# Eight weight buffers moved to different addresses, and half of the matrix products run from the last column to the first

## What is computed

```
for i in range(2):
    x = LN(a*x + 0.5 * swiglu(x, w_gu[i,0], w_down[i,0]))      # 1024 -> 2 x 2816 -> 1024
    y = token_mix(x @ w_in[i]) @ w_out[i]                      # attention heads, recurrent heads
    x = LN(a*x + y)
    x = LN(a*x + 0.5 * swiglu(x, w_gu[i,1], w_down[i,1]))
    x = x + sigmoid(x @ w_g[i] + b_g[i]) * (p[i] @ w_p[i])
```

## Time and profile before

| | |
|---|---|
| median of 2 runs | 2225.23 us (2224.98 to 2225.49) |
| span of the profiled execution | 2226.4 us |
| PE busy | 2188.5 us, 98% of the span |
| weight loads (beside PE) | 1807.6 us, 81% |
| DVE, ACT, POOL busy | 1134.1, 902.1, 137.8 us |
| mean granted TensorE clock | 0.998 of 2.4 GHz |

### The profile page before, as it was taken

How to read it: one execution, slowest core, us unless ns; L and a number is a source line. 1 busy time by engine, 2 the same in 40 slices (tenths; PEclk the granted TensorE clock), 3 DMA queues, 4 the chain that set the end, 5 groups by cost and what they waited for, 6 DMA issues and landing times.

```text
span 2226.4 us, 30811 instructions
## 1 busy us (share of the span) xinstructions
PE 2188.5 (98%) x12675; PEld 1807.6 (81%) x12675; DVE 1134.1 (51%) x1966; ACT 902.1 (41%) x1447; POOL 137.8 (6%) x128
## 2 busy tenths in 40 slices
PE   9999999999999999999999999999999999999999
PEld 7888889877668888888888888898776788888888
DVE  4333345888867333343643333358887663333454
ACT  4223224555656322322632222255466462232234
POOL 0000011210001000012000000112200100000110
PEclk9999999999999999999999999999999999999999
DMA  5333333322222333332333333333322233333322
GB/s 167 97 102 95 88 95 90 99 65 70 81 72 67 104 95 98 106 89 85 107 95 95 100 100 86 98 80 99 77 67 67 67 95 96 101 98 97 95 88 72
DMA packets 384219, 202.76 MB, mean 91 GB/s; under 512 B 17360, under 2 KB 381776, under 8 KB 384080
## 3 DMA queue, kind: packets, MB, share of 16 engines
q1 hardware_dynamic: 383520, 200.15, 31.7%
q10 hardware_dynamic: 560, 0.66, 0.1%
HBM read 198.68 MB, written 2.10 MB: 90 GB/s over the span
## 4 chain that ended last, share of the span: by engine, by line
PE 82%; DVE 9%; ACT 6%; issue 2%; DMA 1%; POOL 0%; SPq 0%; DVEq 0%; ACTq 0%
PE banks L254 24%; PE banks L255 24%; PE banks L256 24%; DVE lev L1241 2%; ACT xhi L353 1%; PE banks L1518 1%; DVE w_lo L246 1%; DVE att L1277 1%; ACT lev L1121 1%; ACT w_hi L240 1%; ACT xT L354 1%; PE banks L1505 1%; PE banks L1459 1%; PE banks L305 1%; PE banks L311 1%
## 5 line engine op out<-in xcount | busy, mean ns | idle before, releaser
L246 DVE TENSOR_TENSOR w_lo<-w_raw,w_hi 128x1024 fp32r<-128x1024 f32 (+2 forms) x370 | 452.5, 1226 | 831.6 <-ACT w_hi L240 831.3
L254 PE MATMUL banks<-xhi,w_hi 128*128 128x512 f32 (+1 forms) x1936 | 758.1, 392 | 1.0 <-DVE w_lo L246 1.0
L256 PE MATMUL banks<-xhi,w_lo 128*128 128x512 f32 (+1 forms) x1936 | 749.7, 387 | 0.0
L255 PE MATMUL banks<-xlo,w_hi 128*128 128x512 f32 (+1 forms) x1936 | 749.7, 387 | 0.0
L240 ACT ACTIVATE w_hi<-w_raw 128x1024 fp32r<-128x1024 f32 (+2 forms) x370 | 376.0, 1018 | 810.0 <-PE banks L256 796.7
L254 PEld LDWEIGHTS banks<-xhi,w_hi 128*128 128x128 f32 x1936 | 365.6, 189 | 75.8 <-issue 1.6
L256 PEld LDWEIGHTS banks<-xhi,w_lo 128*128 128x128 f32 x1936 | 364.1, 188 | 74.6
L255 PEld LDWEIGHTS banks<-xlo,w_hi 128*128 128x128 f32 x1936 | 364.5, 188 | 72.5 <-issue 1.0
L254 PE MATMUL banks<-hhi,w_hi 128*128 128x512 f32 (+1 forms) x792 | 293.4, 371 | 0.0
L256 PE MATMUL banks<-hhi,w_lo 128*128 128x512 f32 (+1 forms) x792 | 289.5, 365 | 0.0
L255 PE MATMUL banks<-hlo,w_hi 128*128 128x512 f32 (+1 forms) x792 | 289.4, 365 | 0.0
(11 more groups left out here) (274 smaller groups left out, 2002.0 us busy)
## 6 DMA issues: line engine op xcount, KB each, us to landing
w_raw<-in_ffn_w_gu_dram SPq DMA_DIRECT2D x176, 512.0 KB, 4.0
w_raw<-in_ffn_w_down_dram SPq DMA_DIRECT2D x64, 512.0 KB, 4.0
w_raw<-in_w_in_dram SPq DMA_DIRECT2D x48, 512.0 KB, 4.1
w_raw<-in_ffn_w_down_dram SPq DMA_DIRECT2D x32, 384.0 KB, 3.5
w_raw<-in_w_out_dram SPq DMA_DIRECT2D x32, 256.0 KB, 2.9
w_raw<-in_ple_gate_w_dram SPq DMA_DIRECT2D x16, 512.0 KB, 3.7
w_raw<-in_cmp_k_w_dram SPq DMA_DIRECT2D x16, 256.0 KB, 2.8
w_raw<-in_cmp_v_w_dram SPq DMA_DIRECT2D x16, 256.0 KB, 3.2
```

Of the source, the lines that this page charges most:

```text
L246: dve.tensor_tensor(part_view(wlo, n), raw_view(split_at[n]).rearrange("p k n -> p (k n)"), part_view(whi, n), ALU.subtract).then_inc(sems ...
L254: pe.matmul(bank, w_hi, x_hi, start=first, stop=False)
L255: pe.matmul(bank, w_hi, x_lo, start=False, stop=False)
L256: return pe.matmul(bank, w_lo, x_hi, start=False, stop=last)
```

## The change

Two things change for the operands of the products.

**Addresses.** Each split buffer gets 64 bytes behind its 4096, so that the four buffers of `w_hi` begin 64 bytes apart modulo 512, and those of `w_lo` follow on: the eight begin at eight different residues modulo 512 (counted from the residue of the moving tiles: 0, 64, 128, 192 for `w_hi` and 256, 320, 384, 448 for `w_lo`). Room comes from `place`, which now reserves two bytes for a 2-byte element, and from `mask_b` and `ident_b` at their used width: 3072 bytes less, of which the buffers take 512. `w_raw` moves down by 3072 bytes and the working tiles behind the buffers by 2560, all by whole multiples of 512. ACT and DVE write the split pieces through a view of blocks (blocks x 128) in place of one run of the same elements, and read the raw piece in the same view.

**Direction.** In `multiply`, for pieces with `n // 4` odd, the moving tiles and the result bank are addressed with step -1: the first column that is read is column 511, and its result goes to column 511 of the bank. The weights are read as before. Nothing changes in what lands where. The other functions with products keep their direction.

```
-            at[0] += 4 * int(np.prod(shape[1:]))
+            at[0] += (2 if dt == BF16 else 4) * int(np.prod(shape[1:]))
...
-        mask_b = place(low, "mask_b", [P, 2 * (C_HG - C_MASK)], BF16)
-        ident_b = place(low, "ident_b", [P, 2 * P], BF16)
+        mask_b = place(low, "mask_b", [P, C_HG - C_MASK], BF16)
+        ident_b = place(low, "ident_b", [P, P], BF16)
...
-        whi = place(low, "w_hi", [P, SPLIT, KT, P], F32R)
-        wlo = place(low, "w_lo", [P, SPLIT, KT, P], F32R)
+        whi = place(low, "w_hi", [P, SPLIT, KT * P + 16], F32R)
+        wlo = place(low, "w_lo", [P, SPLIT, KT * P + 16], F32R)
+        low[0] += (high[0] - low[0]) % (4 * P)
...
         def part_view(t, n):
-            _src, kt, wide, _n, _cmp = stream[split_at[n]]
-            return t[:, n % SPLIT, :, :].rearrange("p k n -> p (k n)")[:, 0:kt * wide]
+
+            return t[:, n % SPLIT, 0:blocks_in(n) * P].rearrange("p (b n) -> p b n", n=P)
+
+        def raw_blocks(n):
+
+            return raw[:, split_at[n] % RAW, 0:blocks_in(n), :]
+
+        def w_of(t, n, b):
+
+            return t[:, n % SPLIT, b * P:(b + 1) * P]
...
-            act.activation(part_view(whi, n), raw_view(c).rearrange("p k n -> p (k n)"), ACT.Copy).then_inc(sems["hi_done"], 1)
+            act.activation(part_view(whi, n), raw_blocks(n), ACT.Copy).then_inc(sems["hi_done"], 1)
...
-            slot = n % SPLIT
             for i, k in enumerate(ks):
                 if ready:
                     ready(k)
-                mm = three(pe, ps[:, bank, :], whi[:, slot, k, :], wlo[:, slot, k, :], hi(k), lo(k),
+                to, x_hi, x_lo = ps[:, bank, :], hi(k), lo(k)
+                if n // SPLIT % 2:
+                    to, x_hi, x_lo = to[:, ::-1], x_hi[:, ::-1], x_lo[:, ::-1]
+                mm = three(pe, to, w_of(whi, n, k), w_of(wlo, n, k), x_hi, x_lo,
                            first and i == 0, last and i == len(ks) - 1)
```

More of the change, by code:

```diff
@@ L198, in raw_view, with blocks_in @@
             return raw[:, c % RAW, :, :].rearrange("p k n -> p (k n)")[:, 0:kt * n].rearrange("p (k n) -> p k n", n=n)
+        def blocks_in(n):
+            _src, kt, wide, _n, _cmp = stream[split_at[n]]
+            return kt * wide // P
         def part_view(t, n):
-            _src, kt, wide, _n, _cmp = stream[split_at[n]]
-            return t[:, n % SPLIT, :, :].rearrange("p k n -> p (k n)")[:, 0:kt * wide]
+            return t[:, n % SPLIT, 0:blocks_in(n) * P].rearrange("p (b n) -> p b n", n=P)
[3 more added lines that the diff above has]
+            return t[:, n % SPLIT, b * P:(b + 1) * P]
         def load_piece(sp, c):
@@ L245, in split_lo @@
             dve.wait_ge(sems["hi_done"], n + 1)
-            dve.tensor_tensor(part_view(wlo, n), raw_view(split_at[n]).rearrange("p k n -> p (k n)"), part_view(whi, n),
+            dve.tensor_tensor(part_view(wlo, n), raw_blocks(n), part_view(whi, n),
                               ALU.subtract).then_inc(sems["lo_done"], 1)
@@ L279, in multiply_first @@
                     for u in range(3):
-                        slot = (n + u) % SPLIT
-                        pe.matmul(ps[:, banks[u], :], whi[:, slot, k, :], xhi[:, k, :], start=(k == 0), stop=False)
-                        pe.matmul(ps[:, banks[u], :], wlo[:, slot, k, :], xhi[:, k, :], start=False, stop=False)
+                        pe.matmul(ps[:, banks[u], :], w_of(whi, n + u, k), xhi[:, k, :], start=(k == 0), stop=False)
+                        pe.matmul(ps[:, banks[u], :], w_of(wlo, n + u, k), xhi[:, k, :], start=False, stop=False)
                 if k:
@@ L285, in multiply_first @@
                     for u in range(3):
-                        slot = (n + u) % SPLIT
-                        mm = pe.matmul(ps[:, banks[u], :], whi[:, slot, k - 1, :], xlo[:, k - 1, :], start=False, stop=(k == DT))
+                        mm = pe.matmul(ps[:, banks[u], :], w_of(whi, n + u, k - 1), xlo[:, k - 1, :], start=False, stop=(k == DT))
                         if k == DT:
@@ L303, in multiply_halves @@
                                 pe.wait_ge(sems["lo_done"], n + u + 1)
-                            slot, to = (n + u) % SPLIT, ps[:, banks[u], cols]
-                            pe.matmul(to, whi[:, slot, k, :], xhi[:, k, cols], start=(k == 0), stop=False)
-                            pe.matmul(to, wlo[:, slot, k, :], xhi[:, k, cols], start=False, stop=False)
+                            to = ps[:, banks[u], cols]
+                            pe.matmul(to, w_of(whi, n + u, k), xhi[:, k, cols], start=(k == 0), stop=False)
+                            pe.matmul(to, w_of(wlo, n + u, k), xhi[:, k, cols], start=False, stop=False)
                     if k:
@@ L309, in multiply_halves @@
                         for u in range(3):
-                            slot = (n + u) % SPLIT
-                            mm = pe.matmul(ps[:, banks[u], cols], whi[:, slot, k - 1, :], xlo[:, k - 1, cols], start=False, stop=(k == DT))
+                            mm = pe.matmul(ps[:, banks[u], cols], w_of(whi, n + u, k - 1), xlo[:, k - 1, cols], start=False, stop=(k == DT))
                             if h == 1 and k == DT:
@@ L452, in last_tile @@
                 k0 = DOWN[part][0]
-                slot = (last + part) % SPLIT
                 for k in ks:
-                    mm = three(pe, ps[:, bank, cols], whi[:, slot, k, :], wlo[:, slot, k, :], hhi[:, k0 + k, cols], hlo[:, k0 + k, cols],
+                    mm = three(pe, ps[:, bank, cols], w_of(whi, last + part, k), w_of(wlo, last + part, k), hhi[:, k0 + k, cols], hlo[:, k0 + k, cols],
                                k0 + k == 0, k0 + k == FT - 1)
@@ L695, in embed_pe @@
                 pe.wait_ge(*upto("p_lo", layer, PT_))
-            hi, lo = (part_view(t, n).rearrange("p (k n) -> p k n", k=PT_) for t in (whi, wlo))
             for j in tiles:
@@ L703, in embed_pe @@
                 for k in range(PT_):
-                    mm = three(pe, ps[:, E_BANK[j], :], hi[:, k, m * P:(m + 1) * P], lo[:, k, m * P:(m + 1) * P],
+                    mm = three(pe, ps[:, E_BANK[j], :], w_of(whi, n, k * len(whole_) + m), w_of(wlo, n, k * len(whole_) + m),
                                phi[:, k, :], plo[:, k, :], k == 0, k == PT_ - 1)
@@ L754, in last_gate @@
                 for k in range(DT):
-                    mm = three(pe, ps[:, LAST_BANK[h], cols], whi[:, slot, k, :], wlo[:, slot, k, :], xhi[:, k, cols], xlo[:, k, cols],
+                    mm = three(pe, ps[:, LAST_BANK[h], cols], w_of(whi, n, k), w_of(wlo, n, k), xhi[:, k, cols], xlo[:, k, cols],
                                k == 0, k == DT - 1)
@@ L1577, in att_piece @@
                 n, k0 = w0 + DT + a % KH, KH * (a // KH)
-                slot = n % SPLIT
                 pe.wait_ge(sems["lo_done"], n + 1)
                 for i, k in enumerate(ks):
-                    mm = three(pe, ps[:, bank, :], whi[:, slot, k0 + k, :], wlo[:, slot, k0 + k, :], xhi[:, k, :], xlo[:, k, :],
+                    mm = three(pe, ps[:, bank, :], w_of(whi, n, k0 + k), w_of(wlo, n, k0 + k), xhi[:, k, :], xlo[:, k, :],
                                first and i == 0, last and i == len(ks) - 1)
@@ L1587, in att_half @@
                 n = w0 + DT + a - KH
-                slot, cols = n % SPLIT, HALVES[h]
+                cols = HALVES[h]
                 pe.wait_ge(sems["lo_done"], n + 1)
                 for k in range(KH):
-                    mm = three(pe, ps[:, bank, cols], whi[:, slot, KH + k, :], wlo[:, slot, KH + k, :], xhi[:, k, cols], xlo[:, k, cols],
+                    mm = three(pe, ps[:, bank, cols], w_of(whi, n, KH + k), w_of(wlo, n, KH + k), xhi[:, k, cols], xlo[:, k, cols],
                                k == 0, k == KH - 1)
@@ L1934, in first_products @@
                 pe.wait_ge(*upto("x_lo", 0, k + 1))
-                mm = three(pe, ps[:, u, :], whi[:, u, k, :], wlo[:, u, k, :], xhi[:, k, :], xlo[:, k, :], k == 0, k == DT - 1)
+                mm = three(pe, ps[:, u, :], w_of(whi, u, k), w_of(wlo, u, k), xhi[:, k, :], xlo[:, k, :], k == 0, k == DT - 1)
             if k == DT - 1:
```

## The result

The changed kernel takes **2258.63 us** (2 runs, 2258.51 to 2258.75) against 2225.23: ratio 1.0149, 95% interval 1.0119 to 1.0178. It is slower by 33 us where no change was forecast. Its profiled execution has a span of 2256.9 us against 2226.4.

The account below looks back on a forecast made before the run. PE was taken as the bound, through the 227 ns interval of 7608 products of 512 columns. The terms summed as 0 + 0 + 0 + 0, so 2225 us was predicted against the median, with a range of 2130 to 2600.

Parts of the forecast that it names:

- the likeliest case: The total for the whole kernel most expected by itself: 2215 to 2242 us.
- What bounds the kernel: PE, busy 98% of the span; 7608 products of 512 columns at 227 ns each, 1727 us or 78%.
- The 64 bytes between the buffers: Weight reads of all 7608 products and the 256-column ones: taken as zero, bounds 101 us faster to 38 us slower.
- the 13 ns: Surplus in each 227 ns interval over 213.3 ns for 512 columns, taken as the cost of changing weights.
- The reversed runs: Descending products in odd rounds of `multiply`, 3690 of 7608: taken as zero, upper bound +738 us.
- the 12 ns: Sign of a wrong prediction: a descending run having any price over 12 ns a product.
- The splits, the layout of the masks, the moved tiles: Split pieces on ACT and DVE in block views, mask layout and shifted working tiles: each taken as zero.
- Half rate: Rival: bank or moving read takes descending columns at half rate in 3690 products, +738 us, 2963 us; chance 0.17.
- The rival of the rhythm: PE's product intervals no longer settle at 227 ns: slower, 2242 to 2263 us; chance 0.08.
- The collision theory: Rival: weight and moving reads collide now and no longer would, 51 to 101 us faster; chance 0.14 of over 2%.
- a mark of an address effect: Expected in the profile: intervals changing with the buffer, period of four pieces, and unreversed 256-column products changing too.

Follow-up runs that it names:

- e1_addresses_alone: Changed kernel with its new addresses kept but every product ascending: 2249.58 us, ratio 1.0100 to the kernel before.
- e2_direction_alone: Changed kernel with all eight buffers at the moving tiles' residue, odd rounds still descending: 2248.56 us, ratio 1.0096 to the kernel before.
- e13_halves_descend: Changed kernel with buffers at distance 0, 512-column products ascending, 256-column products in multiply_halves reading and writing descending: 2226.16 us, before 2227.40.
- e11_steps_of_256: Changed kernel with split buffers at residues 0 and 256 in turn, all ascending, block views and smaller mask tiles kept: 2227.22 us, ratio 1.0005.
- e8_bank_alone_descends: Changed kernel with buffers at distance 0; in odd rounds only the bank is written descending, the moving tile read ascending: 2230.34 us, before 2226.32.
- e7_moving_alone_descends: Changed kernel with buffers at distance 0; in odd rounds only the moving tile is read descending, the bank written ascending: 2248.27 us, before 2226.32.

## Why the prediction was wrong

*The number.* 2258.63 us lies inside the stated range of 2130 to 2600, which was that wide for partly slowed products; the likeliest case, 2215 to 2242, missed it by 17 us. No change was forecast, and the change cost 33 us.

*What bounds the kernel.* Right: one number, the interval of 227 ns, decided, and one ns on it is worth 7.6 us.

*The 64 bytes between the buffers: the step that failed.* I took zero "because the nearest rows with other widths (rows 6) show the same surplus". They do, but they couldn't speak about addresses. Worked out from `place`, `mask_b` and `ident_b` began 3072 bytes apart and the columns used of them 0 or 256 bytes in: also a distance of zero modulo 256. Every row I compared was at distance zero, so none could show what another distance does. In place of zero the runs showed 4.0 ns on each ascending product of the pieces read (`e1_addresses_alone`, 3.6 as the mean of the whole trace, +1.0% in time), from 0 at distance 0 over 6.7 at 32 and 64 to 7.5 at 96. With it falls what I inferred from those rows, that the 13 ns are a fixed cost of changing weights: at other distances the surplus is up to 21 ns at 512 columns, and under 12 at 256.

*The reversed runs: the second term that failed.* I took zero between 0 and +738 us; it is 6.7 ns a product, 3690 of them, 24.6 us by this sum and 21 us as measured (`e2_direction_alone`, +1.0%). That is under the 12 ns which the prediction named as its sign of being wrong, so that sign was set too high. L1008 with its gaps (rows 8) was of no use as the nearest row: its products have 16 columns, and `e13_halves_descend` shows that even 256 columns don't tell of 512.

*The splits, the layout of the masks, the moved tiles.* Right at zero, by `e11_steps_of_256`.

*The rivals.* Half rate didn't happen: the bank takes descending columns at full rate (`e8_bank_alone_descends`), and a descending read loses 6.7 ns and not 200 (`e7_moving_alone_descends`). The rival of the rhythm had the price (2242 to 2263 us), and for the addresses it had the mechanism: I wrote that the relation of weight and moving address may be what lets intervals settle at 227, and in ascending pieces of buffers 1 to 3 they no longer do; they go round in cycles between 225 and 241 ns. I gave it a chance of 0.08. It doesn't cover the descending pieces of the changed kernel, which settle within three products, at 233. That both together fell into its price range is in part luck: its sums were made from other numbers. The view ahead of the prediction that pointed there was rows 5: unchanged addresses, and intervals from 224 to 240 ns (rounded to 0.22 and 0.24 us in the rows). The collision theory's sign was wrong at 512 columns, where distance zero is the best of the eight tried, and right at 256, where spread buffers gain 1.7 ns; that the 256-column products would change too is what the prediction named as a mark of an address effect.

*The pages.* The Trainium skill, "PSUM — Partial Sum Buffer", "Specifications (TRN2)": any access pattern that isn't contiguous slows matmuls. Read strictly, the trace disagrees for a descending run of neighbouring columns: 226.7 ns either way (`e8_bank_alone_descends`). Read by lines of two columns, as the prediction also did, it agrees. The Trainium skill's "TensorE: Matmul & The Clock Gate", under "Step-by-step: what each phase is for", says that loading the next tile's weights doesn't steal read bandwidth from the running matmul. The measurement is not at ease with that: moving the weights' addresses alone, with every product ascending, made those at a distance of 64 bytes 6.7 ns longer (`e1_addresses_alone`). What exactly the two share isn't shown here.

**What stays open.** Which two accesses meet. Shown: the distance between weights and moving tile modulo 256 bytes matters, reading the moving tile from its last column matters at 512 columns, the bank doesn't. Only argued: that it is the weight load beside a product that meets the product's read. No run has the load in the other direction. Not separated either: a descending read also begins elsewhere, 2044 bytes into the tile, 4 bytes short of a multiple of 256. No run moved the tiles or the weights by 4 bytes, so the price of a descending piece may be one of its start and not of its direction. Why 256 columns gain where 512 lose is open too.

## What to carry to other kernels

Where PE is the bound, read its rate from start to start and piece by piece; 7 ns in 227 are invisible in a busy share of 98% or 99% but are 3%. Keep weights and moving tiles of a 512-column stream in the four-byte fast format at the same address modulo 256 bytes, and read the moving tile ascending; a spread of the buffers to different addresses should go in steps of 256. This was seen in one kernel, and for a stream of 256 columns it doesn't hold: there distance zero was the slower one, by 1.7 ns. Before a row is used as a comparison for an edit of addresses, work out its own addresses.

## What the runs showed of the hardware that I had not expected

Only two intervals were seen to stay constant for long stretches at 512 columns, 226.7 and 233.3 ns. They are 6.67 ns apart, 16 cycles of 2.4 GHz. Whether constant intervals come in such steps isn't shown by two of them. Ascending pieces at distances of 64, 128 and 192 bytes stay in cycles instead, with means of 233.3, 232 and 229 ns. Products of 256 columns gain 1.7 ns from the addresses that cost ascending 512-column products 3.6 to 4 in the mean. A bank can be written from last to first column at no cost.
